# A hybrid decoder step on one core: 320 instead of 256 tokens of the expert sums by fetched rows, v's 16 bit parts made a stage earlier, v's largest value found beside the attention, and two seams rearranged

## The reference, cut to what matters

```python
act = jax.nn.gelu(jnp.einsum('thkd,td->thk', peer_u[e], xb))
return jnp.einsum('thk,thkd->td', g * act, peer_v[e])
x = x + gate2 * peer(h)        # and a last RMSNorm
```

## Time and profile before

| | |
|---|---|
| median of 3 runs | 4880.0 us (4876.19 to 4882.35) |
| profiled execution, its own time | 4877.53 us |
| its span in the trace | 4875.6 us |
| PE, DVE, ACT, POOL busy | 4503.4, 2893.8, 1339.6, 910.0 us |
| mean granted PE clock | 0.95 |
| moved by DMA | 854.93 MB |

### The profile page before, as it was taken

How to read it: one execution, slowest core, us unless ns; L and a number is a source line. 1 busy time by engine, 2 the same in 40 slices (tenths; PEclk the granted TensorE clock), 3 DMA queues, 4 the chain that set the end, 5 groups by cost and what they waited for, 6 DMA issues and landing times. The chain is left out here.

```text
span 4875.6 us, 71419 instructions
## 1 busy us (share of the span) xinstructions
PE 4503.4 (92%) x26288; PEld 2714.0 (56%) x26288; DVE 2893.8 (59%) x5214; ACT 1339.6 (27%) x1823; POOL 910.0 (19%) x982
## 2 busy tenths in 40 slices
PE   5999979998767997999999999999996999999995
PEld 2666634443444564666666666666663555555553
DVE  5465313444554445326666666666545898888984
ACT  3232213333111001223444444443222222122221
POOL 0000013321000010000000000000004666666640
PEclk8999989998776998999999999999998999999998
DMA  4533423322323455224645555555447888888861
GB/s 178 188 132 141 158 70 94 86 77 67 104 87 145 149 186 188 74 99 152 210 168 199 188 193 185 180 207 180 154 137 263 306 296 290 302 292 296 298 219 74
DMA packets 397656, 854.93 MB, mean 175 GB/s; under 512 B 42514, under 2 KB 233618, under 8 KB 388562
## 3 DMA queue, kind: packets, MB, share of 16 engines
q1 hardware_dynamic: 274162, 470.37, 28.9%
q0 software_dynamic: 78752, 283.31, 17.1%
q10 hardware_dynamic: 44480, 97.93, 5.4%
HBM read 673.44 MB, written 178.03 MB: 175 GB/s over the span
## 5 line engine op out<-in xcount | busy, mean ns | idle before, releaser
L373 PE MATMUL dot_ps<-h_parts,u_parts 128*128 128x384 f16 (+1 forms) x9216 | 1454.0, 317 | 7.5 <-PEq L1979 4.9
L373 PEld LDWEIGHTS dot_ps<-h_parts,u_parts 128*128 128x128 f16 x9216 | 893.0, 98 | 499.3 <-issue 8.2
L373 PE MATMUL totals_ps<-act_parts,v_parts 128*128 128x416 f16 x6144 | 1084.3, 340 | 37.2 <-DVE act_parts L2900 33.3
L373 PEld LDWEIGHTS totals_ps<-act_parts,v_parts 128*128 128x128 f16 x6144 | 602.0, 98 | 518.2 <-issue 37.0
L386 PE MATMUL in_ps<-h_parts_in,in_parts 128*128 128x384 f16 (+1 forms) x3168 | 492.6, 318 | 4.9 <-DVE in_parts L713 4.5
L2615 DVE SCALAR_TENSOR_TENSOR u_parts<-u_chunks,units,u_parts 128x1024 f16<-128x1024 f32 x126 | 161.8, 1284 | 515.9 <-ACT u_parts L2399 515.9
L2408 ACT ACTIVATE gelu<-dot_ps,units 128x384 f32<-128x384 f32 (+1 forms) x384 | 216.3, 564 | 803.2 <-PE dot_ps L373 803.1
L386 PEld LDWEIGHTS in_ps<-h_parts_in,in_parts 128*128 128x128 f16 x3168 | 309.5, 98 | 182.3 <-DVE in_parts L713 4.6
L2967 POOL DMA_INDIRECT row_value<-tmp_g_rows,row_g x256 | 304.6, 1190 | 394.0 <-POOLq L2273 316.2
L2856 ACT ACTIVATE v_parts<-v_group,units 128x1024 f16<-128x1024 f32 x128 | 136.6, 1139 | 773.5 <-PE totals_ps L373 740.7
L2911 DVE SCALAR_TENSOR_TENSOR h<-totals_ps,sum_unit,h 128x416 f32<-128x416 f32 x388 | 248.0, 648 | 142.0 <-PE totals_ps L373 138.4
(11 more groups left out here) (365 smaller groups left out, 5395.7 us busy)
## 6 DMA issues: line engine op xcount, KB each, us to landing
u_chunks<-in_u SPq DMA_DIRECT2D x128, 512.0 KB, 5.5
v_sweep<-in_v SPq DMA_DIRECT2D x128, 512.0 KB, 4.6
v_group<-in_v SPq DMA_DIRECT2D x32, 2048.0 KB
tmp_g<-gelu ACTq DMA_DIRECT2D x128, 416.0 KB, 2.7
tmp_w<-h POOLq DMA_DIRECT2D x26, 2048.0 KB, 8.2
w_groups<-tmp_w SPq DMA_DIRECT2D x32, 1664.0 KB
gelu_in<-tmp_g SPq DMA_DIRECT2D x32, 1664.0 KB
merge_sweep<-in_u POOLq DMA_DIRECT2D x64, 512.0 KB, 7.7
```

Of the source, the lines that this page charges most:

```text
L373: mm = pe.matmul(bank, left(x), right(y), start=first and x == 0 and y == 0, stop=last and x == 1)
```

## The change

- TD falls from 832 to 768 (6 tiles); the last 320 tokens go by rows: NROWS = 320, in order tile 6, tile 7, and half a group for the 64 samples, whose 128 slots are split over both halves of the partitions. Products are 384 columns wide, the dense table has 24 blocks instead of 26, there are 6 row buffers instead of 5, and every dense tile is a full one.
- v is swept in `attend_phase`: ACT issues two loads of 512 KB in steps 1 to 8 of each head, DVE reduces two in steps 3 to 10, in 8 buffers. The scale of v comes out of `query_phase` with the others.
- In `dots_phase` the sweep is replaced by making v's two parts: per chunk ACT writes the first (after its gelus), DVE the second (last in its chunk), into a single buffer, and SP stores it to HBM (`tmp_v16`), three places later in its own order. ACT waits for the store of the chunk before. SP waits for all stores at the end of the phase.
- `sums_phase` loads the parts ready-made; ACT's and DVE's v parts go. The first group's gelus are loaded in four pieces, the first parts are made piece by piece.
- Seams: in `merge_phase` the squares of both halves come first, each half has its own rstd and banks, the 24 products with the attention's output of a turn come before those with y, and x is loaded again from HBM at the phase's start. `modulated` does the samples of all chunks at once after the loop. The last group of the sums adds x (loaded during the last two groups) and the gate itself, so `final_phase` starts with its squares.

```diff
-TD = (TILES - 1) * P - TS
+TD = (TILES - 2) * P
-NROWS = 2 * FULL
+NROWS = 2 * FULL + FULL // 2
@@ modulated
     for k in range(KC):
         dve.tensor_tensor(dst[:, k, :], src[:, k, :], s["rstd"][:, :], ALU.mult).then_inc(scaled, 1)
-        dve.wait_ge(scaled, k + 1)
-        own = dst[:, k, SEQ:T].rearrange("p (s l) -> p s l", l=LS)
-        link(dve.tensor_tensor(own, own, per_seq(gain, k), ALU.mult))
-        dve.tensor_tensor(own, own, per_seq(sh, k), ALU.add)
+    dve.wait_ge(scaled, KC)
+    own = dst[:, :, SEQ:T].rearrange("p k (s l) -> p k s l", l=LS)
+    link(dve.tensor_tensor(own, own, per_seq(gain), ALU.mult))
+    dve.tensor_tensor(own, own, per_seq(sh), ALU.add)
@@ attend_phase, vector
+                def sweep(i, u, j):
+                    m = i * (2 * PER_HEAD) + (u * PER_HEAD + j)
+                    dve.wait_ge(vs_in[j % RV], i * (2 * 16 * PER_HEAD // RV) + 16 * (u * PER_HEAD // RV + j // RV + 1))
+                    ...
+                    dve.tensor_reduce(out, v_sweep[:, j % RV, :], AX.X, ALU.max,
+                                      apply_absolute_value=True).then_inc(v_swept, 1)
...
                         sample(i, u, n)
+                        if 0 <= n - 3 < PER_HEAD // 2:
+                            sweep(i, u, 2 * (n - 3))
+                            sweep(i, u, 2 * (n - 3) + 1)
@@ attend_phase, scalar
+                        if n <= PER_HEAD // 2:
+                            load_sweep(i, u, 2 * (n - 1))
+                            load_sweep(i, u, 2 * (n - 1) + 1)
@@ merge_phase
+                sp.dma_start(x[:, :, :], a["x"]).then_inc(x_back, 16)
...
                 group[0].tensor(pe)
-                pe.wait_ge(y_ready, 1)
                 group[1].tensor(pe)
-                pe.wait_ge(y_ready, 2)
...
+                        if u == 0:
+                            pe.wait_ge(y_ready, KC)
+                        for j, (t0, n) in enumerate(SPLITS):
                             for k in range(KC):
@@ dots_phase, sync
+                def store_v(at, late):
+                    sp.wait_ge(v_made, at.chunk(off=1 - late))
+                    ...
+                    sp.dma_start(to, v_parts).then_inc(v_out, 16)
...
+                for late in range(LATE - 1, -1, -1):
+                    store_v(tail(TAIL - 1), late)
+                sp.wait_ge(v_out, 16 * NK)
@@ dots_phase, scalar
+                def lead_v(at):
+                    r = at.n % 2
+                    act.wait_ge(v_in[r], at.chunk(16, 0, 2) + 16)
+                    if at.i is not None or at.n >= 1:
+                        act.wait_ge(v_out, at.chunk(16))
+                    act.activation(v_parts[:, 0, :], v_in32[:, r, :], ACT.Copy,
+                                   scale=units[:, V_SCALE:V_SCALE + 1]).then_inc(v_lead, 1)
@@ dots_phase, vector
-                    dve.tensor_reduce(out, swept[:, r, :], AX.X, ALU.max,
-                                      apply_absolute_value=True).then_inc(v_swept, 1)
+                    dve.wait_ge(v_lead, at.chunk(off=1))
+                    dve.scalar_tensor_tensor(v_parts[:, 1, :], v_in32[:, r, :], units[:, V_SCALE:V_SCALE + 1],
+                                             v_parts[:, 0, :], ALU.mult, ALU.subtract).then_inc(v_made, 1)
@@ sums_phase
-        RR, BATCH = 5, 8
+        RR, BATCH = 6, 8
...
-                    sp.dma_start(v[:, r, :, :], a["v"][g]).then_inc(v_in[r], 16)
+                    sp.dma_start(v16[:, r, :, :, :], src).then_inc(v_in[r], 16)
...
-                                rest_v(n, o, (2 * m - 4, 2 * m - 3))
-                            elif m < 6:
-                                rest_a(n, o, (2 * m - 8, 2 * m - 7))
+                                rest_a(n, o, (2 * m - 4, 2 * m - 3))
                         add(g, m)
+                        if g == LAST:
+                            for k in GATED_AT.get(m, ()):
+                                gated(k)
```

More of the change, by code:

```diff
@@ L211, with __init__ @@
 class Norm:
-    def __init__(self, nc, sem, name, src, squares, s, psum, chunks=KC):
+    def __init__(self, nc, sem, name, src, squares, s, psum, chunks=KC, rstd=None):
         self.nc, self.src, self.sq, self.s, self.psum, self.chunks = nc, src, squares, s, psum, chunks
+        self.rstd = s["rstd"] if rstd is None else rstd
         self.squared = sem(name + "_squared")
@@ L222, in __init__, with squares @@
         self.scaled = sem(name + "_scaled")
-    def scalar(self, act, loaded=None):
+    def squares(self, act, loaded=None):
         for k in range(self.chunks):
@@ L228, in scalar, with roots @@
             act.activation(self.sq[:, k, :], self.src[:, k, :], ACT.Square).then_inc(self.squared, 1)
+    def scalar(self, act, loaded=None):
+        self.squares(act, loaded)
+        self.roots(act)
+    def roots(self, act):
         for i, (t0, n) in enumerate(SPLITS):
             act.wait_ge(self.meaned, i + 1)
-            r = self.s["rstd"][:, t0:t0 + n]
+            r = self.rstd[:, t0:t0 + n]
             act.activation(r, r, ACT.Sqrt).then_inc(self.rooted, 1)
@@ L863, in attend_phase @@
         o_s = sb("o_sample", [P, NC_, TS])
+        RV, PER_HEAD = 8, NK // HEADS
+        v_sweep = sb("v_sweep", [P, RV, D])
+        vs_in = [sem(f"v_row_read{r}") for r in range(RV)]
+        v_swept, vs_passed = sem("v_swept"), sem("v_sweep_passed")
         zs = ctx.enter_context(nc.psum_tensor("z_ps", [P, 4, 512], F32))
@@ L1821, in merge_phase @@
         HALF_C = KC // NG
+        rstds = [s["rstd"], sb("rstd_group", [P, T])]
         group = [Norm(nc, sem, f"group{g}", y[:, g * HALF_C:(g + 1) * HALF_C, :],
-                      h[:, g * HALF_C:(g + 1) * HALF_C, :], s, ps, HALF_C) for g in range(NG)]
+                      h[:, g * HALF_C:(g + 1) * HALF_C, :], s, ps[:, g * NS:(g + 1) * NS, :], HALF_C, rstds[g])
+                 for g in range(NG)]
         norm = Norm(nc, sem, "norm2", x, y, s, ps)
@@ L1897, in _ @@
             def _(act):
-                group[0].scalar(act)
-                act.wait_ge(y_ready, 1)
-                group[1].scalar(act)
+                group[0].squares(act)
+                group[1].squares(act)
+                group[0].roots(act)
+                group[1].roots(act)
                 act.wait_ge(mix_taken, KC + 2)
@@ L2788, in _ @@
                 load_w(0, 0)
-                load_g(0)
+                for j in range(GRP):
+                    sp.dma_start(gl[:, j, :], a["g"][j]).then_inc(first_in[j], 16)
                 load_v(0, 0)
@@ L2792, in _, with load_x @@
                 load_v(1, 1)
+                def load_x():
+                    for k in range(KC):
+                        sp.dma_start(x_late[:, k, :], a["x_mid"][:, k, :]).then_inc(x_in, 16)
                 def turn(g, r, i):
@@ L2865, in turn @@
                         parts(g + 1, 1 - r, i + r)
-                parts(0, 0, 0)
+                first_parts()
                 rounds(act, turn)
@@ L2954, in _ @@
                 dve.sem_inc(row_added, 1)
-                weigh(0, 0, 0, range(GRP))
-                rest_v(0, 0, range(GRP))
-                rest_a(0, 0, range(GRP))
+                for j in range(GRP):
+                    weigh(0, 0, 0, (j,))
+                    if j > 0:
+                        rest_a(0, 0, (j - 1,))
+                rest_a(0, 0, (GRP - 1,))
                 for g in range(NGRP):
@@ L2999, in _ @@
             def _(sp):
-                for k in range(KC):
-                    sp.dma_start(x[:, k, :], a["x_mid"][:, k, :]).then_inc(x_in, 16)
                 for k in range(KC):
```

267 lines of the change are left out of this document (134 added, 133 removed).

## The result

The changed kernel takes 4915.2 us (median of four runs, 4903.7 to 4920.2) where the kernel before took 4880.7 in the same session (4876.2 to 4882.4). The ratio is 1.0069, 95% interval 1.0056 to 1.0082: slower by 34.5 us, where 76 us less were forecast. It lies above the range, 4765 to 4875.

The account below looks back on a forecast made before the run. PE was taken as the bound, busy nearly throughout dots and sums. Terms -7 + 45 - 19 + 0.5 - 9.9 - 6 - 64 - 15.5 = -76 took 4877.5 to 4801.5, as a median 4804 us; range 4765 to 4875.

Parts of the forecast that it names:

- The sums: Sums stage: POOL's row path at 2.99 us a row sets 31.9 us a group, 0.6 over PE; -64 us.
- the row path makes it slower than before: Rival, sums: rows come late and PE stands, 3.4 us a row, 36.3 us a group; 4936 us, chance 0.08.
- PE's price: Sums: a product of 384 columns takes 163 ns by columns instead of 176.5, 31.3 us a group; -83 us by itself.
- The rule weighed: Sums: if DVE leaves descriptor generation alone, a row costs 2.5 us and hides; trace speaks against, unless offset reads are held.
- Attention: Attention: 128 added DVE reductions of v lengthen steps without room, 11.5 us a pair of heads, 8 the first; +45 us.
- Merge: Merge seam: half 1's statistics ready early, PE does attention-output products first, y ends at 1586.2 instead of 1596.1; -19 us.
- second norm: Norms: DVE's small products moved behind the loop cut ACT's step pitch to 1.24 us; 3.4 us, twice, -7 in all.
- seam: Dots to sums: phase ends 4.5 us later, but the first group's parts are ready near 3713 instead of 3719.2; -6 us.
- end: After PE's last product: the gate lies in the last group, last squares start about 12 us after PE's end; -15.5 us.
- a row path at 2.99 us or less: Sums: the forecast at 2.99 us a row, chance 0.48, and the rival of a hidden path, 4786 us, chance 0.17.
- The start of the sums: Sums, first groups: 6 us allowed for everything loading at once, making 1025.6 us against 1089.
- Dots: Dots: 128 fewer one-hot products on PE at 77 ns, v's parts and stores costing PE nothing; -9.9 us.

Follow-up runs that it names:

- experiment 5: The changed kernel with 256 fetched rows and 832 dense tokens as before, all else of the change kept: 4870.2 us, ratio 0.9988 to the kernel before.
- experiment 4: The changed kernel with each row fetch cut to 512 columns and DVE's row addition replaced by a one-operand reduction: 4780.2 us, ratio 0.9801.
- experiment 1: The changed kernel without the 320 value fetches in the sums; row fetches, their bytes and DVE's additions stay: 4783.5 us, ratio 0.9805.
- Experiment 3: The changed kernel with DVE's addition of each fetched row replaced by a reduction with one SBUF operand, fetches kept: 4868.8 us, ratio 0.9983.
- Experiment 8: The kernel of experiment 6 with row fetches begun only when the second group's gelu block has landed: 4857.0 us, ratio 0.9958.
- experiment 9: The kernel of experiment 8 with 288 tokens by fetched rows and 800 in the dense part: 4813.0 us, ratio 0.9871.
- experiment 6: The kernel of experiment 5 with v's reductions beside attention moved into steps where DVE was seen idle, loads following: 4867.8 us, ratio 0.9977.
- experiment 7: The changed kernel with each of v's 128 reductions beside attention reading 16 columns instead of 1024, loads kept: 4902.3 us, ratio 1.0041.

## Why the prediction was wrong, step by step

**The sums: the failed step.** "I take 2.99, the good stretch with a little waiting: 31.9 us a group." A row costs 3.3 us of POOL and a group 35.8. Three things in that step:
- The price, 2.91 and a little for waiting, came from a stretch in which POOL had slack, though the run's own mean, 3.18, stood beside it. Even that was no upper bound: the values' fetches went from 1.19 to 1.34 us.
- v's rest (the second float16 part, L2894) was indeed one of the instructions that held POOL: without it the pair costs 2.97 us at 256 rows (experiment 5, both means and two gaps), with it 3.18. But the price was taken as fixed, and it rises with the rows: 2.97 at 256, 3.11 at 288, 3.33 at 320, each row bringing an addition of 1.28 us that holds what starts under it. The traces split the rise: at 256 rows 46% of the fetches begin under two operands from SBUF, at 288 rows 60%, at 320 rows 63%; these take 1.48, 1.45 and 1.60 us. So up to 288 rows more fetches are caught, and from there to 320 each is held longer. That the longer holds come from DVE working back to back once a late row has come fits the 3.68 us above, but was not tested.
- The rival that came true was written down: "the row path makes it slower than before", 3.4 us a row, 36.3 us a group, 4936, deciding from 3.26 on. Mechanism and place are as told; it had a chance of 0.08. The stretch at 3754 us, in which POOL never waited, was the nearer of the two rows, because the change makes all of the stage like it. With its 1.41 us an operation the sum would have come to 4936, 21 too much.

PE's price was right: 0.163 us a product (experiment 4: 1848 products in 300 us are 0.162). In the changed kernel PE's busy time is 1035.9 - 1001.5 = 34 us more than that, at a mean granted clock of 0.97: after a wait for a bank some products run at the lower of its two clocks, 1.2 GHz (a granted clock of 0.50 from 4091 to 4093 us, behind the wait of 4.78). The idle time is 107 us. Some 17 us of it fall before 3760 us, at the start of the stage, and with 256 rows the stage has 15 in all (experiment 5); so some 90 came with the rows.

**The bytes were no limit.** The estimate of 338 GB/s, beside 340 needed, was too low as a bound: experiment 1 ran at 349 with PE full. The number was given as a second reason for 31.9 us and did not carry the sum.

**The rule weighed.** Experiment 3 decides it. The Trainium skill, SBUF — State Buffer, section "Who interferes with whom", infers that descriptor generation is left alone by DVE's instructions with two SBUF inputs; here fetches of 1.34 and 1.39 us fell to 1.07 and 1.02 when one kind of these instructions was replaced by one with a single SBUF input, of nearly the same length. The measurement decides against that inference for these fetches: they are held. It does not speak against the rule of the same section that a DVE instruction with two SBUF inputs contends with a GpSimd instruction that reads SBUF. A fetch here takes its offsets from SBUF, which the prediction named as the way out; whether it is this read that is held, no run here tests. The forecast did weigh the rule and went with the trace, but then priced the trace's effect too low.

**Attention: mechanism right, size too large.** The stretch of 12.4 us went to 18.3 (19.0 forecast), the one of 4.9 to 8.9 (9.1), which answers to the earlier trace rows:

```profile
981.70:1000.00 18.30, 17.05 (x44) 6.32 (x42) 17.97 (x31) 9.10 (x16) 7.78 (x15) 0.91 1.00 330
1037.60:1046.50 8.90, 7.78 (x34) 3.79 (x32) 8.76 (x18) 4.95 (x9) 0.00 (x0) 1.00 0.97 317
```

DVE is full in both. But the steps around them gave some back, since PE then had less left to do there: a pair of heads grew by 8.4 us, not 11.5 (60.7 + 66.9 against 55.4 + 63.8, third and fourth head), and the first pair by 1.7 instead of 8. Attention itself, from PE's first product to its last, grew by 27.2 us (501.7 to 528.9), just over the lower bound, 25. The 23.5 of the table holds the scan behind it as well, which took 3.7 us less; no run says why.

**Merge, second norm, seam, end: right.** -18.9, -2.0, -7.5 and -15.6 against -19, -3.5, -6 and -15.5. y's first product starts at 1605.5 us, 37.6 after the stage's start at 1567.9, as the steps had it (1586.2, with the start at 1548.6 before). In the end the last squares answer to the earlier trace rows:

```profile
4861.48 8.10 ACT L232 ACTIVATE squares_end<-h 128x1088 f32<-128x1088 f32 x8 [14.19 <-PEq L2813]
```

They start 11.3 us after PE's last product; 12 was forecast.

**The start of the sums: mis-sized by 14.** 6 us were allowed for loading at once. The windows of the changed kernel:

```profile
3700.00:3720.00 20.00, 11.33 (x60) 6.29 (x60) 7.51 (x9) 1.93 (x3) 15.73 (x15) 0.80 1.04 369
3720.00:3740.00 20.00, 7.08 (x27) 3.53 (x28) 9.50 (x12) 3.60 (x4) 6.25 (x5) 0.57 0.89 291
3740.00:3760.00 20.00, 20.00 (x125) 12.05 (x124) 18.02 (x22) 0.46 (x1) 16.64 (x12) 1.00 0.92 293
```

212 products in the 55 us from 3705 on, 34.6 us at 0.163: 20 lost, while the transfers ran at up to 369 GB/s. Experiment 8 got 9 us back, on the kernel with 256 rows, by letting the first rows wait; how much of the 20 that would be here was not run. In experiment 5, too, the earlier start of the stage is lost here.

**Dots: -6.2 instead of -9.9.** A one-hot product among the others was priced at 77 ns. Between experiment 5 and the changed kernel 128 of them make 7.1 us, 55 ns each, if all of the difference is theirs; v's parts and stores in place of the sweep cost 0.9 us in all (experiment 5 against before).

**The chances.** The forecast's cases were right in kind and wrong in weight: 0.65 lay on a row path at 2.99 us or less, about its price in a stretch with slack.

## What to carry to other kernels

When a change gives more work to an engine that now has slack, price it by the stretches in which it has none, however few, and ask what else changes once it starts its instructions back to back. Where two limits are close (here PE at 31.3 us a group, POOL at 35.5), look for the split between them instead of an all or nothing: 288 rows beat 256 by 44 us with nearly all else the same (experiments 8 and 9), and lie 102 under the changed kernel with its 320, of which experiments 6 and 8 explain some 13. Work that "has room" in the mean of a stage has to be put into the steps that have it. And a seam that starts a stage earlier gains nothing if the stage then waits for its own loads.

## What the runs showed that was not expected

- POOL's indirect fetches, of 4 bytes or of 4 KB a descriptor, take 0.94 us while DVE stands or reads one operand from PSUM, and 1.60 in the mean when they begin under an instruction of DVE that reads two operands from SBUF: they end 0.8 us behind it, which in a chain of such instructions made 3.68.
- With transfers at 317 GB/s in both large and very small packets, PE's products can come 0.70 us apart with no wait in the program; the same rows at 349 GB/s without the small fetches showed none of it, and neither did 327 GB/s with both (experiments 1, 3, 4 and 9). What PE waits for there is not shown.
- 64 MB of loads beside attention, at a DMA share that went from 0.29 to 0.67, cost it 0.6 us (experiment 7).
- At POOL's pace the sums took 1145 us in one profiled execution and 1168 in another with the same code in that stage.
